# Four normed residuals in two pieces of 256 tokens: sum, root and the next block's first rows by halves

## What is computed

```python
def rms_norm(x, g):
    xf = x.astype(jnp.float32)
    y = xf * lax.rsqrt(jnp.mean(xf * xf, axis=-1, keepdims=True) + EPS)
    return (y * g.astype(jnp.float32)).astype(x.dtype)
...
    x = x + rms_norm(f, norm_ffn_post[layer])
```

## Time and profile before

| what | value |
|---|---|
| median of 3 runs | 2582.3 us (2581.4 to 2582.34) |
| the profiled execution: time, span | 2581.04 us, 2579.2 us |
| PE busy | 2554.8 us (99%) |
| DVE busy | 1663.2 us (64%) |
| ACT busy | 1275.3 us (49%) |
| POOL busy | 361.5 us (14%) |

### The profile page before, as it was taken

The page is one execution under the profiler, slowest core; times in us unless marked ns, Lnnn a source line. Parts: engine busy times, 40 slices in busy tenths (PEclk is TensorE's granted clock), DMA queues, the critical chain, the costliest instruction groups (busy, mean ns, idle before and its releaser), DMA issues.

```text
span 2579.2 us, 35285 instructions
## 1 busy us (share of the span) xinstructions
PE 2554.8 (99%) x12630; PEld 2028.7 (79%) x12630; DVE 1663.2 (64%) x2398; ACT 1275.3 (49%) x2142; POOL 361.5 (14%) x270
## 2 busy tenths in 40 slices
PE   9999999999999999999999998999999999999999
PEld 7855788888787557788888775799988777899887
DVE  4476677643988895677653777597633546687533
ACT  4326543333546895444333578577533425567432
POOL 0020100000103782100000130000610002000800
PEclk9999999999999999999999999999999999999999
DMA  5330232222243442232233230132232231332222
GB/s 215 106 94 25 92 102 98 97 93 95 84 134 121 136 132 74 80 100 98 98 98 98 95 103 1 61 120 99 90 108 94 95 101 50 98 123 99 82 98 98
DMA packets 74833, 250.44 MB, mean 97 GB/s; under 512 B 8764, under 2 KB 9148, under 8 KB 74336
## 3 DMA queue, kind: packets, MB, share of 16 engines
q1 hardware_dynamic: 73632, 240.63, 28.5%
q0 software_dynamic: 944, 8.33, 0.9%
q10 hardware_dynamic: 144, 0.00, 0.0%
HBM read 242.50 MB, written 2.24 MB: 95 GB/s over the span
## 4 chain that ended last, share of the span: by engine, by line
PE 92%; DVE 3%; ACT 2%; issue 1%; DMA 1%; SPq 0%; POOL 0%; DVEq 0%; ACTq 0%; POOLq 0%
PE bank L432 25%; PE bank L433 24%; PE bank L434 24%; PE bank L1361 2%; PE bank L1363 2%; PE bank L1362 2%; PE bank L2257 2%; PE bank L654 1%; PE bank L639 1%; PE bank L3153 1%; PE bank L1706 1%; PE bank L2807 1%; PE bank L640 1%; PE bank L1695 1%; PE bank L2264 1%
## 5 line engine op out<-in xcount | busy, mean ns | idle before, releaser
L383 DVE TENSOR_TENSOR wlo<-wraw,whi 128x1024 fp32r<-128x1024 f32 x344 | 441.2, 1284 | 447.1 <-ACT whi L360 446.5
L360 ACT ACTIVATE whi<-wraw 128x1024 fp32r<-128x1024 f32 x348 | 366.5, 1055 | 506.9 <-DMA wraw<-in_w 506.8
L432 PE MATMUL bank<-hnhi,whi 128*128 128x512 f32 (+1 forms) x1528 | 596.4, 390 | 1.1 <-DVE wlo L383 0.7
L433 PE MATMUL bank<-hnlo,whi 128*128 128x512 f32 (+1 forms) x1528 | 584.5, 383 | 0.0
L434 PE MATMUL bank<-hnhi,wlo 128*128 128x512 f32 x1392 | 542.1, 389 | 0.0
L432 PE MATMUL bank<-ahi,whi 128*128 128x512 f32 x1184 | 463.6, 392 | 1.8 <-DVE stats L2916 0.6
L434 PE MATMUL bank<-ahi,wlo 128*128 128x512 f32 x1184 | 460.8, 389 | 0.0
L433 PE MATMUL bank<-alo,whi 128*128 128x512 f32 x1184 | 460.7, 389 | 0.0
L432 PEld LDWEIGHTS bank<-hnhi,whi 128*128 128x128 f32 x1528 | 287.2, 188 | 86.5 <-issue 29.9
L433 PEld LDWEIGHTS bank<-hnlo,whi 128*128 128x128 f32 x1528 | 287.4, 188 | 57.3 <-issue 3.4
L434 PEld LDWEIGHTS bank<-hnhi,wlo 128*128 128x128 f32 x1392 | 261.3, 188 | 55.6
(11 more groups left out here) (360 smaller groups left out, 3935.9 us busy)
## 6 DMA issues: line engine op xcount, KB each, us to landing
wraw<-in_w SPq DMA_DIRECT2D x410, 512.0 KB, 3.3
arena<-cs_scratch SPq DMA_DIRECT2D x20, 512.0 KB, 6.1
over_a<-cs_scratch SPq DMA_DIRECT2D x12, 512.0 KB, 5.9
arena<-in_rpb POOLq DMA_DIRECT2D x1, 2880.0 KB, 13.9
arena<-in_t_step POOLq DMA_DIRECT2D x2, 897.0 KB, 5.3
mT<-arena SPq DMA_DIRECT2D x28, 64.0 KB, 2.0
out_dram<-xT SPq DMA_DIRECT2D x7, 256.0 KB, 2.0
arena<-in_t_ab POOLq DMA_DIRECT2D x1, 1472.0 KB, 6.5
```

Of the source, the lines that this page charges most:

```text
L360: act.activation(whi[:, slot * BLOCK:(slot + 1) * BLOCK], wraw[:, slot * BLOCK:(slot + 1) * BLOCK], ACT.Copy).then_inc(sem("w_hi"), 1)
L383: dve.tensor_tensor(low_home(i), wraw[:, slot * BLOCK:(slot + 1) * BLOCK], whi[:, slot * BLOCK:(slot + 1) * BLOCK], ALU.subtract).then_inc ...
L432: pe.matmul(out, wh, ah, start=start, stop=False)
L433: pe.matmul(out, wh, al, start=False, stop=False)
```

## The change

The last block of the four output products runs in two pieces: tile 0 whole, then tiles 1 to 7 for tokens 0 to 255, then tiles 1 to 7 for tokens 256 to 511, and squares, adds, sum over partitions and root are made for each piece. Both sums land in bank 0. The sum over partitions takes two matmuls in place of three, since DVE now adds six squares. The last half of the weight block moves behind the first two rows. In the next product, the first two rows are used in two pieces against blocks 0 and 1 (`pe_up_early`), and their high and low parts are made and counted in pieces. The five matmuls of `pe_busy` are gone.

```diff
-                    if n in POSTED and m == 0:
-                        act.wait_ge(sem("post_unit"), POST_UNITS * (n - 1) + 2)
-                        act.activation(hn_parts(0)[0][:, 0:HALF], xt(0)[:, 0:HALF], ACT.Copy, scale=col(g, g0))
-                    if n in POSTED and m == 1:
-                        act.wait_ge(sem("post_unit"), POST_UNITS * (n - 1) + 5)
-                        act.activation(hn_parts(1)[0][:, 0:HALF], xt(1)[:, 0:HALF], ACT.Copy, scale=col(g, g0 + 1))
...
+        def row_done(n, m, first=False):
+            base = 8 * n + 2 * sum(p < n for p in POSTED)
+            return base + m + 1 + (0 if n not in POSTED or first else 2)
...
+            early = 2 if norm in POSTED else 0
+            if early:
+                pe_up_early(pe, b0, norm, early)
+            for s in range(max(early - 1, 0), KT + max(lags[-1], 1)):
...
+        def pe_up_early(pe, b0, norm, early):
+
+            def term(b, k, c, w, a):
+                pe.matmul(bank[b][:, c:c + HALF], w_parts(At(b0 + b), k * P)[w], hn_parts(k)[a][:, c:c + HALF],
+                          start=k == 0 and w == 0 and a == 0 and c == 0, stop=False)
+
+            for b in range(2):
+                pe.wait_ge(sem("w_lo"), b0 + b + 1 + extra(b0))
+            pe.wait_ge(sem("post_rstd"), 2 * norm)
+            for c in HALVES:
+                for k in range(early):
+                    pe.wait_ge(sem("norm_hi"), row_done(norm, k, c == 0))
+                    for b in range(2):
+                        term(b, k, c, 0, 0)
+                        term(b, k, c, 1, 0)
+                for k in range(early):
+                    pe.wait_ge(sem("hn_ready"), row_done(norm, k, c == 0))
+                    for b in range(2):
+                        term(b, k, c, 0, 1)
...
+        def pe_down_last(pe, name, K, d):
+
+            def half(m, c):
+                a = (K - 1) % 2 * SEQ + c
+                out, (wh, wl) = bank[m][:, c:c + HALF], w_parts(At(FIRST[name] + K - 1), m * P)
+                pe.matmul(out, wh, ahi[:, a:a + HALF], start=False, stop=False, skip_group_check=bool(c))
+                pe.matmul(out, wh, alo[:, a:a + HALF], start=False, stop=False, skip_group_check=bool(c))
+                return pe.matmul(out, wl, ahi[:, a:a + HALF], start=False, stop=True, skip_group_check=bool(c))
+
+            pe.wait_ge(sem("a_lo"), A0[name] + K)
+            pe.wait_ge(sem("w_lo"), FIRST[name] + K + extra(FIRST[name]))
+            pe_product(pe, name, At(K - 1), 0).then_inc(sem("down_done"), 1)
+            for m in range(1, KT):
+                half(m, 0).then_inc(sem("down_done"), 1)
+            for m in range(1, KT):
+                pe.wait_ge(sem("post_sq"), squared(d, 0, m))
+                half(m, HALF).then_inc(sem("down_done" if m < KT - 1 else "w_used"), 1)
+                if m == 3:
+                    pe_post_sum(pe, d, 0)
+            pe_post_sum(pe, d, 1)
...
         def act_post(act, name, K, d):
+            third = At(FIRST[name] + K + 2)
+            g, g0 = NORM_G[d + 1]
+
+            def square(i, m):
+                c = HALVES[i]
+                wait_half(act, name, K, d, i, m)
+                act.activation(post_sq(m, i), bank[m][:, c:c + HALF], ACT.Square).then_inc(sem("post_sq"), 1)
+
+            def log(i):
+                act.wait_ge(sem("post_sum"), 2 * d + i + 1)
+                act_order(act, act.activation(rstd[:, HALVES[i]:HALVES[i] + HALF], post_sum(i), ACT.Ln, bias=const(EPS),
+                                              scale=1.0 / DM))
+
+            def root(i):
+                r = rstd[:, HALVES[i]:HALVES[i] + HALF]
+                act.activation(r, r, ACT.Exp, scale=-0.5).then_inc(sem("post_rstd"), 1)
+
+            def early(m):
+                act.wait_ge(sem("post_unit"), POST_UNITS * d + 2 * m + 2)
+                act.activation(hn_parts(m)[0][:, 0:HALF], xt(m)[:, 0:HALF], ACT.Copy, scale=col(g, g0 + m))\
+                    .then_inc(sem("norm_hi"), 1)
+
             act_split(act, At(FIRST[name] + K + 1))
-            for m in range(KT):
-                wait_down(act, name, K, d, m)
-                act.activation(post_sq(m), bank[m][:, :], ACT.Square).then_inc(sem("post_sq"), 1)
-            act_split_half(act, At(FIRST[name] + K + 2), 0)
-            act_split_half(act, At(FIRST[name] + K + 2), 1)
-            for c in HALVES:
-                act.wait_ge(sem("post_sum"), 2 * d + (1 if c == 0 else 2))
-                act_rsqrt(act, post_squares(c), rstd[:, c:c + HALF], 1.0 / DM, EPS, "post_rstd")
-
-        def pe_post(pe, d):
-            for c in HALVES:
-                pe.wait_ge(sem("post_scaled"), 2 * d + (2 if c else 1))
-                for m in (KT - 2, 0, KT - 1):
-                    if m == 0:
-                        pe.wait_ge(sem("post_added"), d + 1)
-                    else:
-                        pe.wait_ge(sem("post_sq"), 8 * d + m + 1)
-                    mm = pe.matmul(post_squares(c), ones, post_sq(m)[:, c:c + HALF], start=m == KT - 2, stop=m == KT - 1)
-                mm.then_inc(sem("post_sum"), 1)
-            pe.wait_ge(sem("post_rstd"), 2 * d + 1)
-            pe_busy(pe, bank[0], 5)
-
-        def pe_busy(pe, out, n):
-
-            for _ in range(n):
-                pe.matmul(out[:, 0:2 * P], ones, base_t[:, 0:2 * P], start=True, stop=True)
+            wait_half(act, name, K, d, 0, 0)
+            act.activation(over_hn[:, 0:SEQ], bank[0][:, :], ACT.Square).then_inc(sem("post_sq"), 1)
+            for m in range(1, KT):
+                square(0, m)
+            for m in range(1, 4):
+                square(1, m)
+            act_split_half(act, third, 0)
+            log(0)
+            square(1, 4)
+            root(0)
+            for m in range(5, KT):
+                square(1, m)
+            early(0)
+            log(1)
+            root(1)
+            early(1)
+            act_split_half(act, third, 1)
...
+        def pe_post_sum(pe, d, i):
+            if i:
+                pe.wait_ge(sem("post_rstd"), 2 * d + 1)
+            else:
+                pe.wait_ge(sem("post_scaled"), 2 * d + 1)
+            pe.wait_ge(sem("post_added"), 2 * d + i + 1)
+            pe.matmul(post_sum(i), ones, post_sq(0, i), start=True, stop=False)
+            pe.wait_ge(sem("post_sq"), squared(d, i, KT - 1))
+            pe.matmul(post_sum(i), ones, post_sq(KT - 1, i), start=False, stop=True).then_inc(sem("post_sum"), 1)
...
         def dve_post(dve, name, K, d, g, g0):
-            dve_split(dve, At(FIRST[name] + K + 1))
-            dve.wait_ge(sem("post_sq"), 8 * d + 1)
-            dve.tensor_scalar(mt(0), bank[0][:, :], col(g, g0), None, ALU.mult).then_inc(sem("post_scaled"), 1)
-            dve.wait_ge(sem("post_scaled"), 2 * d + 1)
-            for m in range(1, KT - 2):
-                dve.wait_ge(sem("post_sq"), 8 * d + m + 1)
-                ins = dve.tensor_tensor(post_sq(0), post_sq(0), post_sq(m), ALU.add)
-                if m < KT - 3:
+            third = At(FIRST[name] + K + 2)
+            ng, ng0 = NORM_G[d + 1]
+
+            def add(i, m):
+                dve.wait_ge(sem("post_sq"), squared(d, i, m))
+                ins = dve.tensor_tensor(post_sq(0, i), post_sq(0, i), post_sq(m, i), ALU.add)
+                if m < KT - 2:
                     dve_order(dve, ins)
                 else:
                     ins.then_inc(sem("post_added"), 1)
-            dve.tensor_scalar(mt(1), bank[1][:, :], col(g, g0 + 1), None, ALU.mult).then_inc(sem("post_scaled"), 1)
-            for part in range(2):
-                dve_split_half(dve, At(FIRST[name] + K + 2), part, 2 * d + 1)
-            dve.wait_ge(sem("post_scaled"), 2 * d + 2)
+
+            def scaled(m):
...
+            dve_split(dve, At(FIRST[name] + K + 1))
+            dve.wait_ge(sem("post_sq"), squared(d, 0, 0))
+            scaled(0)
+            for m in range(1, KT - 1):
+                add(0, m)
+            for m in range(1, 4):
+                add(1, m)
+            scaled(1)
+            dve_split_half(dve, third, 0, 2 * d + 1)
+            dve.wait_ge(sem("post_scaled"), 2 * d + 2)
             unit(0, 0)
+            for m in range(4, KT - 1):
+                add(1, m)
             added(0, 0, 1)
             unit(1, 0)
+            added(1, 0, 3)
+            early_low(0)
             unit(0, HALF)
-            added(0, HALF, 4)
-            added(1, 0, 3)
+            added(0, HALF, 5)
+            early_low(1)
             unit(1, HALF)
             added(1, HALF, 6)
+            dve_split_half(dve, third, 1)
             for m in range(2, KT + 2):
                 if m == 3:
                     dve.wait_ge(sem("post_unit"), post_unit(d, 2))
@@ -897,7 +999,10 @@
                 if m < KT:
                     dve.scalar_tensor_tensor(out=mt(m), in0=bank[m][:, :], scalar=col(g, g0 + m), in1=rstd[:, :],
                                              op0=ALU.mult, op1=ALU.mult).then_inc(sem("post_unit"), 1)
-                dve_low(dve, d + 1, m - 2)
```

(4 more changed lines are left out.)

45 lines of the change are left out of this document (33 added, 12 removed).

## The result

| | before | changed |
|---|---|---|
| median of 6 runs on the same chip, us | 2581.93 (2581.27 to 2582.59) | 2593.69 (2591.17 to 2595.18) |
| ratio, 95% interval | | 1.0044 [1.0034, 1.0053] |
| profiled execution, us / its span | 2581.04 / 2579.2 | 2593.83 / 2592.0 |
| mean granted clock of TensorE | 1.00 | 0.996 |
| TensorE busy, matmul records | 2554.8 us, 12630 | 2551.7 us, 12706 |

The change costs 11.8 us by the medians and 12.8 us by the two spans. 9.6 were forecast.

A forecast was written before the change was run, and what follows sets the result against it. VectorE's list was taken to bound the stretch at each residual, TensorE's pitch the rest. A loss of 2.4 us at each of four residuals, 9.6 in all, on 2582.3 gave 2591.9; range 2586.5 to 2599.0.

The forecast's parts named there:

- 2: first sum starts: Last block: VectorE's six chained adds end at 4.84, so TensorE starts the first sum at 4.96 us.
- 3: first root done: ACT's logarithm and exponential after the first sum finish the first root at 7.22, 1.0 us earlier than before.
- 5: second sum starts: VectorE's second-half adds end at 9.05; second sum starts at 9.17, second root done at 11.14, 1.6 us later than before.
- 6: bank 2 taken up: VectorE's list behind the adds, including early low parts, takes up bank 2 at 13.73, 2.27 us later than before.
- step 8: Next product: at 16.84 TensorE has issued 12 matmuls' worth against 22 before; 2.4 us lost at each residual.
- step 7's first sentence: Next product: TensorE starts row 0 at 10.05, before the old 11.10, with 24 pieces to issue.
- early low parts: VectorE's low parts in pieces, made before bank 2, add 0.74 us to its delay; waits give 0.3 back.
- the clock: Rival, chance 0.08: TensorE's idle gaps at the residuals drop its clock, adding 6.8 us, to 2598.7.
- The four stretches alike: Sign of a right forecast: the stretches at the four residuals behave the same.
- The early start comes through: Rival, chance 0.13: TensorE's earlier start on the next product wins 1.2 us per place, giving 2577.6.
- The chained adds are cheap: Rival, chance 0.11: VectorE's chained 256-column adds go at 0.35 us, giving 2588.3.

The follow-up runs named there:

- e1: Changed kernel with filler matmuls put back ahead of the second sum, behind it and ahead of the last low piece; median 2590.44 us, ratio 1.0036.
- e9: Kernel before with only the next product's first two rows' high parts issued early in pieces, three of five filler matmuls kept; ratio 0.9998.
- e7: Changed kernel with sums and roots in two pieces but the next product's rows whole; ratio 1.0046 without filler, 1.0033 with it.
- e3: Changed kernel without three VectorE adds of the second piece (their squares left out), with filler in two places; ratio 1.0016.
- e2: Changed kernel without three VectorE adds of the second piece (their squares left out), no filler; ratio 1.0032.
- e5: Kernel before with its five filler matmuls at each residual removed, nothing else; median 2583.62 us, ratio 1.0008.
- e6: Kernel before with only the next product's first two rows' high parts issued early in pieces, no filler; ratio 1.0004.
- e8: Changed kernel with the next product's rows whole, three late adds moved to TensorE, and five filler matmuls behind the second sum; ratio 1.0027.
- e4: Changed kernel with three adds of the second piece moved from VectorE to TensorE matmuls, with filler; ratio 1.0026.

## Why the prediction was right, point by point

The forecast was 2591.9, slower, in a range of 2586.5 to 2599.0; measured 2593.69. In us from the zero of each trace:

| step | forecast | measured |
|---|---|---|
| 2: first sum starts | 4.96 | 5.04 |
| 3: first root done | 7.22 | 7.37 |
| 5: second sum starts | 9.17 | 9.30 |
| 5: second root done | 11.14 | 11.37 |
| 6: bank 2 taken up | 13.73 | 13.99 |
| 6: last low piece starts | 16.03 | 16.31 |
| 7: TensorE takes it | 16.60 | 16.84 |
| 8: lost per place, clock full | 2.40 | 2.40 |

- **Right: what sets the time.** That the first root comes earlier (7.37 against 8.20) and the second later (11.37 against 9.50), that VectorE's list decides, and that filler and the sum matmul saved cost and gain nothing by their own length, is as written. The adds were priced at 0.45 from a pair of other operations, and are at 0.45 (3 in 1.34 us). The remark on the Trainium skill (VectorE: DVE Perf Modes, The DRAIN you can't avoid) can be closed with it: a semaphore between chained instructions costs something here, since pieces of that size are 0.35 apart where nothing is waited for the earlier trace rows.
- **Mis-sized: step 8, twice, with opposite signs.** The list ran 0.28 later than worked out at the last low piece (16.31 against 16.03) and 0.24 where TensorE takes it, and e1's first whole matmul behind it starts at 17.18. From there TensorE is 2.7 behind, not 2.36: before, it starts the 23rd matmul at 16.75; e1 has ten to go at 17.18, and 17.18 + 10 x 0.227 - 16.75 = 2.70. But the kernel before loses 0.1 when it restarts at row 3 (the second matmul there starts at 293.83, 0.33 behind the first, where 0.23 is the pitch), and it waits again at the end. Its last matmul of this part and the norm's sum:

```profile
306.78 0.39 PE L434 MATMUL bank<-hnhi,wlo 128*128 128x512 f32 x1
307.21 1.12 PE L515 MATMUL bank<-mT,base_t 128*128 128x512 f32 x2
```

  and the same two in e1, where the sum is line 513:

```profile
309.00 0.40 PE L434 MATMUL bank<-hnhi,wlo 128*128 128x512 f32 x1
309.23 1.02 PE L513 MATMUL bank<-mT,base_t 128*128 128x512 f32 x2
```

  Before, the two are 0.43 apart, 0.2 more than the pitch; e1 is late enough that nothing is waited for. So 2.70 - 0.1 - 0.2 = 2.40. "It runs at its pitch as before" was not so, and the hit on 2.40 owes a part to two errors that cancel.
- **Wrong, without consequence: step 7's first sentence.** TensorE was to begin row 0 at 10.05. `pe_up_early` waits for `post_rstd` at 2 * norm, which is the second root of the residual, and begins at 11.62 (288.65, released by line 893). The last low piece decides in either case. e9 has the same wait, but there the second root is done as early as before, so it shows what the start would be worth: row 0 at 10.04, and nothing won.
- **Right in size of parts:** early low parts 0.4 forecast (0.74 less 0.3 of waits), 0.27 by e7; three of the adds 1.35 (3 x 0.45), 1.44 by e3.
- **Missed: the clock.** I gave it 0.08 as a rival and priced it at 6.8 us on top, from the kernel's first matmuls. (These do run at the lower level, by their pitch: 0.43 apart up to 4.5 us and 0.21 from 4.7 on. The granted clock of the windows view reads 1.00 there all the same, so in the first 5 us of this trace it is not to be relied on.) It came on top of the forecast, at 3.2 us. The step that failed is the argument against it: one gap of 1.84 us followed by full pace does not speak for a stretch that holds gaps of 0.61, 1.74, 1.22, 0.30, 0.37 and 1.15 one behind the other. It does not even speak for itself: behind this same gap the clock fell in six of the eleven traces that have it (last paragraphs of this part). The price of 1.7 per place, a whole stretch of low clock, was near for two places (1.48, 1.37) and wrong for the others, where the same fall came while TensorE had little to issue. "The four stretches alike" was wrong for this reason alone; in e1 they are.
- **The early start comes through:** refuted by e9 in its own terms. The start is earlier by 1.06 us, and from row 3 on no matmul is. The rival's point of decision (the last low piece ready by 14.1) was never near: 16.31. (Its time is 2577.5 by its own 4 x 1.2, not 2577.6.)
- **The chained adds are cheap:** refuted, 0.45.

One thing lies outside the four places. The spans of e1, e2, e3, e5, e6, e8 and e9 are 0.6 to 1.8 us longer than their places account for, and that of e4 is 0.8 shorter. A cause of the longer ones can be seen, and it is the clock again, at the very gap of the earlier trace rows. In the kernel before, the eight attention matmuls behind its 1.84 us take 1.99 us and the next eight start 6.21 behind them (1554.70, 1560.91). In e1:

```profile
1563.40 3.50 PE L2923 MATMUL bank<-arena 64*128 64x512 f32 x8 [1.84 <-DVE stats L3032]
...
1571.13 1.14 PE L2923 MATMUL bank<-arena 64*128 64x256 f32 x8 [0.95 <-DVE stats L3032]
```

The granted clock is 0.52 from 1563 to 1565, and the distance is 7.73 in place of 6.21, 1.5 us lost. The same fall, with eight matmuls in 2.88 to 3.68 us, is in the traces of e2, e3, e6, e8 and e9 (1.6 to 1.7 us each) and a few us earlier in e5 (0.7); it is not in those of before, changed, e4 and both of e7. None of the edits touches this part, and the gap is 1.84 us in all but e5 (1.15). The runs of the kernel before beside e1 would fit: nine with a mean granted clock of 1.000 took 2580.2 to 2581.3 us, seven with 0.999 took 2581.7 to 2582.8; no trace of them was kept. What is left besides is at most 1.2 us in a trace, either way, and stays open. This is why single traces are compared here by places and not by spans.

## What to carry to other kernels

A value needed earlier is worth only what the engine that makes it can still deliver: before cutting a reduction in two to start the first half sooner, count what the cut adds to the list of the engine that already hands over the work, and look one wait further than the one removed. Price parts with TensorE's clock held, by filler in every gap that the edit opens, and price the filler apart; without that e2 put the adds at 1.1 in place of 1.44, and e7 looked dearer than the whole change. One trace in which the clock held behind a gap does not show that the gap is harmless. Where four places of a program do the same work, compare them with each other first: that they differ was the first sign of a second cost.

## What the runs showed of the hardware that was not expected

**The clock fell behind idle time that I had thought too short, and not each time.** In four places with the same gaps (0.6, 1.74 and 1.22 to 1.25 us, then TensorE's pieces) the granted clock of the changed kernel fell at three different points. In the first and fourth it was 0.50 behind the last low piece (294.00 to 297.00; 0.51 from 1458 to 1461), where TensorE has work without end, and cost 1.48 and 1.37 us. In the third place it fell just ahead of row 0, whose first matmul is at 1082.87 (0.53 from 1082 to 1083):

```profile
1080.00:1083.00 3.00, 1.23 (x5) 0.84 (x5) 2.25 (x6) 1.82 (x5) 0.00 (x0) 0.84 0.49 172
1083.00:1085.00 2.00, 2.00 (x10) 2.00 (x11) 1.93 (x6) 1.29 (x3) 0.00 (x0) 0.50 0.03 8
1085.00:1087.00 2.00, 2.00 (x11) 2.00 (x11) 2.00 (x5) 1.29 (x4) 0.00 (x0) 0.50 0.00 0
1087.00:1088.50 1.50, 1.34 (x7) 1.04 (x6) 1.50 (x3) 1.23 (x2) 0.74 (x1) 0.50 0.00 0
1088.50:1090.00 1.50, 1.50 (x8) 1.29 (x8) 1.50 (x3) 0.81 (x2) 1.50 (x2) 0.87 0.00 0
```

That is twice as long at 1.2 GHz, nearly 7 us, and it cost 0.37: the slower matmuls filled the time in which TensorE would have waited for VectorE's low pieces (it waits 0.16 for the last one there, 1.15 in the first place). In the second place the clock was low from 659 to 662, for the same 3 us as in the first, and cost nothing: it was over before the last low piece, for which TensorE still waits 1.12 there. So what a fall costs in these places depends on whether TensorE has more work ready than the low clock can issue, not on its length. The Trainium skill (TensorE: Matmul & The Clock Gate, HAM oscillation) warns of bursts of matmuls with idle gaps between them. The trace agrees that they drop the clock to half (0.50). The waits in the section's example are longer than any gap here: in the changed kernel the clock fell with none over 1.74 us, in e5 with one of 2.56. That it can also spare a place, with the same gaps (e5's second, e2's fourth, and the attention gap in five traces of eleven), no run here explains. The runs of the changed kernel are 4 us apart (2591.17 to 2595.18), the five of e1 1.2; but 25 runs of the kernel before, with its filler, are 3.8 us apart (2579.85 to 2583.63), so it is not shown that the falls at the residuals make that spread.

**Filler of little size held it.** In the seven kernels that have filler at the residuals (the kernel before and six others) the clock was 1.00 in all 28 places; in the five that have none it was so in 4 of 20. The filler was three to five matmuls behind the (second) sum, in e1 and e7 four more ahead of that sum, and in e1, e3 and e4 three (1.46 us) ahead of the last low piece. It need not fill a gap: in e9 three matmuls stand in the stretch where the kernel before has five. It held the clock where it stood and not beyond: the traces of e1, e3, e8 and e9 lost it at the attention gap.
